# Attention in a hybrid mixer block: the query tiles in the order 7, 0, 6, 1, 5, 2, 4, 3 instead of 7 down to 0

## The reference

```python
def block(i):                         # i: query tile, t: its 128 positions
    sc = einsum('bqgrd,bngd->bqgrn', qb, kc) * scale      # "cmp": 63 compressed keys
    pc = softmax(where(c_end <= t, sc, NEG)); o_c = pc @ vc
    ...
    ss_ = qb @ ksel * scale           # "slc": all 16 blocks of 64 keys are chosen, so
    ps = softmax(where(kpos <= t, ss_, NEG)); o_s = ps @ vsel     # this is causal attention
    ...
    sw = qb @ kwb * scale             # "win": the last 512 keys
    pw = softmax(where(wmask, sw, NEG)); o_w = pw @ vwb
o = gt0 * o_c + gt1 * o_s + gt2 * o_w
```

## Time and profile before

| | |
|---|---|
| time, median of 3 runs | 2167.56 us (2167.45 to 2167.75) |
| the profiled execution's own time | 2167.75 us |
| its span, first to last instruction | 2165.9 us |
| TensorE busy | 2071.0 us, 96% of the span |
| VectorE, ScalarE, GpSimd busy | 1190.7, 764.1 and 248.9 us |
| mean granted TensorE clock | 0.975 of full speed |

### The profile page before, as it was taken

The page is one execution under the profiler, slowest core; times in us unless marked ns, Lnnn a source line. Parts: engine busy times, 40 slices in busy tenths (PEclk is TensorE's granted clock), DMA queues, the critical chain, the costliest instruction groups (busy, mean ns, idle before and its releaser), DMA issues.

```text
span 2165.9 us, 28340 instructions
## 1 busy us (share of the span) xinstructions
PE 2071.0 (96%) x9866; PEld 1669.9 (77%) x9866; DVE 1190.7 (55%) x1856; ACT 764.1 (35%) x1206; POOL 248.9 (11%) x210
## 2 busy tenths in 40 slices
PE   4989979799899999999999999999999999999998
PEld 3956659566588888888788888887788888888886
DVE  6647756477422233233533342535977777777777
ACT  4445654456422111122321232323333333333232
POOL 1002230022200000000000000003511111111110
PEclk7979989899999999999999999999999999999999
DMA  6010000000011211121112111321111211211122
GB/s 171 1 40 1 1 17 1 1 1 1 15 44 53 59 47 41 49 68 34 36 47 68 44 44 44 98 101 39 49 58 39 58 48 58 58 44 53 48 58 88
DMA packets 148711, 99.02 MB, mean 46 GB/s; under 512 B 22203, under 2 KB 140173, under 8 KB 148621
## 3 DMA queue, kind: packets, MB, share of 16 engines
q1 hardware_dynamic: 148621, 97.85, 15.8%
HBM read 93.64 MB, written 4.19 MB: 45 GB/s over the span
## 4 chain that ended last, share of the span: by engine, by line
PE 90%; DVE 5%; ACT 2%; issue 2%; POOL 1%; DMA 0%; SPq 0%; DVEq 0%; ACTq 0%; POOLq 0%; PEldq 0%
PE bank L1946 11%; PE bank L1947 11%; PE bank L1948 11%; PE bank L2099 11%; PE bank L2107 6%; PE bank L2108 6%; PE bank L2109 6%; PE bank L2048 4%; PE bank L1848 2%; PE bank L1870 2%; PE bank L1875 2%; PE bank L1891 1%; PE bank L1871 1%; PE bank L1893 1%; PE bank L1892 1%
## 5 line engine op out<-in xcount | busy, mean ns | idle before, releaser
L1946 PE MATMUL bank<-actT_h,ring_h 128*128 128x512 f32 x832 | 325.1, 391 | 4.1 <-DVE ring_l L1357 4.1
L1947 PE MATMUL bank<-actT_l,ring_h 128*128 128x512 f32 x832 | 324.6, 390 | 0.0
L1948 PE MATMUL bank<-actT_h,ring_l 128*128 128x512 f32 x832 | 324.6, 390 | 0.0
L1357 DVE TENSOR_TENSOR ring_l<-raw,ring_h 128x1024 fp32r<-128x1024 f32 x84 | 102.7, 1223 | 339.5 <-ACT ring_h L897 339.3
L1624 DVE TENSOR_TENSOR x<-x,bank 128x1024 f32<-128x1024 f32 x176 | 212.4, 1217 | 38.7 <-PE bank L2099 38.4
L1946 PEld LDWEIGHTS bank<-actT_h,ring_h 128*128 128x128 f32 x832 | 156.8, 189 | 37.1 <-issue 4.5
L1948 PEld LDWEIGHTS bank<-actT_h,ring_l 128*128 128x128 f32 x832 | 156.7, 188 | 32.9
L1947 PEld LDWEIGHTS bank<-actT_l,ring_h 128*128 128x128 f32 x832 | 156.8, 188 | 32.3
L897 ACT ACTIVATE ring_h<-raw 128x1024 fp32r<-128x1024 f32 x84 | 88.6, 1055 | 125.8 <-PE bank L1948 123.2
L867 ACT ACTIVATE pT<-bank 128x512 f32<-128x512 f32 (+1 forms) x148 | 88.2, 596 | 117.6 <-PE bank L1875 114.1
L1316 DVE TENSOR_REDUCE nmx<-bank 128x1 f32<-128x512 f32 (+4 forms) x154 | 95.4, 638 | 60.0 <-PE bank L1850 46.9
(11 more groups left out here) (331 smaller groups left out, 4215.1 us busy)
## 6 DMA issues: line engine op xcount, KB each, us to landing
raw<-in_w_in SPq DMA_DIRECT2D x60, 512.0 KB, 3.8
raw<-in_w_up SPq DMA_DIRECT2D x44, 512.0 KB, 4.9
wd_raw<-in_w_down SPq DMA_DIRECT2D x22, 512.0 KB, 3.5
raw<-in_w_branch SPq DMA_DIRECT2D x32, 256.0 KB, 2.7
x_in<-in_x SPq DMA_DIRECT2D x8, 512.0 KB, 8.2
raw<-in_w_o SPq DMA_DIRECT2D x8, 512.0 KB, 3.5
x<-in_x SPq DMA_DIRECT2D x8, 512.0 KB, 10.1
out<-x SPq DMA_DIRECT2D x8, 512.0 KB, 3.1
```

The source lines that it names most:

```text
L1357: nc.vector.tensor_tensor(dst, src, hi.bitcast(F32), ALU.subtract).then_inc(pl_done, 1)
L1946: nc.tensor.matmul(o, wh(k), ah[:, k, cols], start=k == 0, stop=False)
L1947: nc.tensor.matmul(o, wh(k), al[:, k, cols], start=False, stop=False)
L1948: ins = nc.tensor.matmul(o, wl(k), ah[:, k, cols], start=False, stop=k == k_tiles - 1)
```

## The change

The constant that gives the order of the query tiles takes one tile from the top and one from the bottom in turn.

```diff
-TILE_ORDER = list(range(TT - 1, -1, -1))
+TILE_ORDER = [t for pair in zip(range(TT - 1, TT // 2 - 1, -1), range(TT // 2)) for t in pair]
```

## The result

Over 20 runs of each kernel the change took 2172.12 us (median, 2171.22 to 2176.15) against 2167.7 us, a ratio of 1.0019 with a 95% interval of 1.0013 to 1.0025: slower by 4.4 us, with the whole interval above 1. The forecast was 2168.0 us with a range to 2172.0, so the time lies 0.1 us outside the range's upper end. The kernel before came out 0.14 us above the 2167.56 that the forecast started from; set against it, the change lies on that end. A change of 0.4 us was forecast and 4.4 were measured.

A forecast was written before the change was run, and what follows sets the result against it. TensorE, dense from slot 12, was taken as the limit. Finals +1.5, drain net -1.2 and burst -0.1 gave +0.2 us a group, twice: +0.4, 2168.0 us in terms of the median, range 2164.0 to 2172.0.

The forecast's parts named there:

- What bounds the kernel: From slot 12 to the end of the units, TensorE is the limit and does the same products in either order.
- The drain: From the last unit's first scores (time T) to the last final: 8.7 us instead of 11.02, 2.3 earlier.
- turn 3w: In the drain, the turn of tile 3's w units starts at T+4.3, T being the last unit's first scores.
- T is later: Work that left the drain now lies before T, the last unit's first scores: 1.1 us a group later.
- The burst: Eight pieces in one slot, moved from slot 11 to 14: same price of 4.76 us, started about 0.1 sooner.
- The finals in between: Finals of tiles 0, 1, 4 and 7 wait for GpSimd's sums: 2.8 us instead of 1.26, 1.5 more a group.
- The spread excess: Consecutive turns in slots 16 to 20 and paired pieces in 30 to 35: nothing, the latter at worst 0.5 a group.
- The rule weighed: Two-input VectorE and GpSimd SBUF instructions block each other wholly: finals would lose some 4 us a group more, not 1.5.
- the 3.4 row: Tile 4's measured time from cmp turn to final without a shift, 3.4 us, taken as the price of such finals.
- The clock: Rival: after the moved burst a clock fall comes in group two (+1.5) or vanishes from group one (-1.5); chance 20%.
- Slower: sums and remainders collide: Rival: uncovered sum chains all take 4.17, finals lose 5.3 a group: +5.4, 2173; with part of the clock, 15%.
- Faster: Rival: GpSimd's chain is hidden behind TensorE at all four places, the drain's gain stands alone: -4.9, 2162.7; chance 7%.

The follow-up runs named there:

- experiment 4: Changed kernel with tile 0's extra factor (L1337) multiplied into the gate once before the slots: 2171.98 us, ratio 1.0019.
- experiment 7: Changed kernel with only the tile order replaced, by 7, 0, 6, 5, 4, 3, 2, 1: 2168.79 us, ratio 1.0003.
- experiment 1: Changed kernel with eight buffers instead of four for gated results and each final two slots later: 2164.17 us, ratio 0.9981.

## Why the prediction was right and where it was off

The forecast change was too small by 4 us, and only the width of the range came near the time. Most of the terms were right, one was not.

**What bounds the kernel:** right. TensorE is dense in all slots but those named; over slots 10 to 72 the unexplained excess is 1.9 and 2.25 us of some 130.

**The drain:** right, 8.74 and 8.72 us for 8.7, and each step of it: turn 3w at T+4.33, the last turn 1.45 behind, 2.96 from there to the final.

**T is later:** right, +1.23 for +1.1.

**The burst:** right, 4.64 us for "about 0.1 sooner" than 4.76.

**The finals in between:** the step that failed, by size. The mechanism and the three tiles were right. With tile 7 their sum was forecast as 2.8 and is 4.12 a group; without it, 2.6 and 3.98 (tile 7's small excess is in the ledger's spread row):

| | forecast | measured excess |
|---|---|---|
| tile 7, slot 19 | 0.2 | 0.14 |
| tile 0, slot 22 | 0.7 | 1.55 |
| tile 1, slot 40 | 1.5 | 1.68 |
| tile 4, slot 70 | 0.4 | 0.75 |

Two errors made the 1.55. I took the extra factor of tile 0 (L1337) out of the old drain and did not put it in at slot 22, where tile 0 went: 0.23 and its hand-off. And "VectorE's remainder runs in every slot there but no shift does" was false for tile 0: the shift of 1s, whose last piece is in slot 20, ran from 193.18 to 194.52, just when its result was gated. Experiments 4 and 7 show that it holds VectorE's small step up by 0.6. The rest, at tiles 0 and 4, is that both sums ran at 1.05 to 1.21 where I assumed one slow sum, from the 3.4 of the earlier trace rows; measured are 3.82 at tile 4 and 3.93 with the extra factor in experiment 7, so about 3.7 to 3.8 is the price without a shift. I chose the row at the favourable end of 3.4 to 4.17 because it had the least disturbance, and the trace of before showed why it did not fit. VectorE's list at tile 4, then at tile 3, before the change:

```profile
256.58 0.42 DVE L1342 TENSOR_TENSOR o_gated<-bank,wgt 128x256 f32<-128x256 f32 x1
256.93 1.01 DVE L1316 TENSOR_REDUCE nmx<-bank 128x1 f32<-128x384 f32 x2
257.85 0.68 DVE L1308 TENSOR_TENSOR pT_l<-pT,pT_h 128x512 fp32r<-128x512 f32 x1
...
275.60 0.42 DVE L1342 TENSOR_TENSOR o_gated<-bank,wgt 128x256 f32<-128x256 f32 x1
275.94 1.83 DVE L1308 TENSOR_TENSOR pT_l<-pT,pT_h 128x512 fp32r<-128x512 f32 x2
```

At tile 4 two maxima of pieces stood between the gating and the remainder, so that the first sum ran alone. At tile 3 the slot had no pieces and the remainder followed the gating at once. In the change the slots behind the turns of tiles 0 and 4 (21 and 69) have no pieces either, so the row with two slow sums was the nearer one.

**The spread excess** of +0.34 a group was costed at nothing; slots 10, 16, 19 and 53 have 0.1 each, where pieces, turns and finals meet. The waits by which the prediction would have been wrong did not come: in slots 15 to 20 TensorE waits for no other engine (waits, 176.5 to 193 us), and in slots 30 to 35 neither.

**The rule weighed.** The Trainium skill, SBUF — State Buffer, "Who interferes with whom", would have put the finals at some 4 us a group more than before, measured are 2.7, and by the 3.4 row 1.5. The traces agree with the rule's wait itself: in experiment 4 a VectorE step ended 0.02 us behind GpSimd's instruction. Of the 320 sums in the ten profiles of this study, the 142 that began while a remainder ran took 1.05 to 1.24 us and ended 0.58 to 0.60 us behind that remainder; the other 178 took 0.72 to 0.75. So a sum waits for what is left of the remainder. The worst case taken in the prediction, a whole remainder of 0.67 for each sum, was not reached: a part of the remainder was over when a sum began, and the sum then ended some 0.6 us behind it, not 0.72.

**The rivals.** The clock: falls after the burst were seen in 6 of the 18 groups profiled with a burst of eight, in either order; with such a fall the slot after it took 1.2 to 1.6 us longer (3.50 for 2.34, 3.94 for 2.40). Falls like these may well be part of the scatter between runs of one kernel, which is not shown; they do not explain the change, since the profile after had no such fall and was slower. The Trainium skill, TensorE: Matmul & The Clock Gate, Part 1, says that activity releases the throttle. The traces agree so far that each of the six falls stood behind a burst in which TensorE had waited between pieces; twelve bursts of the same kind were followed by none. "Slower: sums and remainders collide" was the rival that came nearest: the finals lost 3.98 a group (4.12 with tile 7), where it asked for more than 4.7 and I forecast 2.8. "Faster" was refuted by the waits, and experiment 1 shows how much it was about: with all finals hidden the new order takes 2164.2.

What stays open: 0.7 of the 4.4 us lies in no row of the ledger. The profiles differ by 0.8 us ahead of the first scores and by 1.1 in what follows the attention, where both kernels run the same instructions; in the ten profiles that last stretch takes from 1587.6 to 1589.3 us.

## What to carry to other kernels

When a dense engine is the limit, a new order of work changes nothing in it; price each place where the engine depends on a side chain, by the distance that the order leaves and the length of the chain, including what stands ahead of it, and right behind its steps, in the side engines' lists. A chain measured while it was hidden or lucky is too cheap a price for one that is exposed. If the order gains at the end and loses in between, make the distance longer (two slots and four more buffers here were worth 8 us) before judging the order.

## What the hardware showed that was not expected

A VectorE step on 128x4 elements took 0.80 us, and in its place another took 0.79, while GpSimd ran a 1.34 us instruction; both take 0.16 to 0.23 alone. In the ten profiles 404 of the 498 steps of these two kinds took 0.16 to 0.23 us; each of the other 94 took 0.24 to 0.80 and ended 0.02 to 0.03 us behind the end of a GpSimd sum or shift. GpSimd's sum of 128x256 took 0.72 to 0.75 us when it began beside no remainder of VectorE and 1.05 to 1.24 when it did. The clock stood at 1.2 GHz, half, for some 3.4 us after the burst in some executions and at 2.4 GHz in others of the same program.
